# Seven block products per group in the down projection, behind a weight ring of eight

## What is computed

```python
gate, up = _split(rms_norm(x, norm_ffn[i]) @ w_gate_up[i], (D_FF, D_FF))
x = x + (jax.nn.silu(gate) * up) @ w_down[i]
```

## Time and profile before

| what | us |
|---|---|
| median of 3 runs | 2176.54 (2176.45 to 2178.01) |
| the profiled execution, own time | 2178.24 |
| its span, first to last instruction | 2176.4 |
| gate/up loop, layer 0 and 1 | 428.10, 428.33 |
| down projections, layer 0 (with the start of the next stage), layer 1 | 245.11, 239.51 |
| TensorE, VectorE, ScalarE busy in the span | 2158.2, 1555.4, 1095.3 |

### The profile page before, as it was taken

How to read it: one execution, slowest core, us unless ns; L and a number is a source line. 1 busy time by engine, 2 the same in 40 slices (tenths; PEclk the granted TensorE clock), 3 DMA queues, 4 the chain that set the end, 5 groups by cost and what they waited for, 6 DMA issues and landing times.

```text
span 2176.4 us, 29853 instructions
## 1 busy us (share of the span) xinstructions
PE 2158.2 (99%) x10052; PEld 1784.3 (82%) x10052; DVE 1555.4 (71%) x1937; ACT 1095.3 (50%) x1414; POOL 58.4 (3%) x99
## 2 busy tenths in 40 slices
PE   8999999999999999999999999999999999999999
PEld 6888888888888888888888888888878888888887
DVE  6657766888888885555566767677888888874443
ACT  7755654545555554444444444454454545544332
POOL 2101100000000000000100000000000000000000
PEclk9999999999999999999999999999999999999999
DMA  8765466667666666666555656566676666666664
GB/s 313 233 194 155 138 211 204 202 194 222 202 206 214 214 217 199 205 205 202 177 172 164 202 158 191 172 206 209 195 221 203 205 208 217 201 219 218 202 203 133
DMA packets 244569, 435.57 MB, mean 200 GB/s; under 512 B 23040, under 2 KB 43648, under 8 KB 244480
## 3 DMA queue, kind: packets, MB, share of 16 engines
q1 hardware_dynamic: 243392, 432.31, 63.7%
q10 hardware_dynamic: 1088, 2.10, 0.2%
HBM read 411.25 MB, written 2.10 MB: 190 GB/s over the span
## 4 chain that ended last, share of the span: by engine, by line
PE 70%; DVE 11%; issue 7%; SPq 6%; DMA 4%; ACT 2%; DVEq 1%; ACTq 0%
PE unit_bank L1801 52%; SPq L408 5%; PE mix_bank L1853 4%; PE mix_bank L1801 4%; DMA raw<-in_w_gate_up 4%; PE unit_bank L1853 3%; DVE w_lo L1074 3%; PE unit_bank L1813 1%; PE mix_bank L1813 1%; PE mix_bank L1871 1%; DVE sums L1096 1%; ACT w_hi L615 1%; PE mix_bank L2001 1%; DVE up_ff L1574 1%; DVE act_ff L1598 1%
## 5 line engine op out<-in xcount | busy, mean ns | idle before, releaser
L1074 DVE TENSOR_TENSOR w_lo<-raw,w_hi 128x1024 fp32r<-128x1024 f32 x687 | 828.8, 1220 | 472.8 <-ACT w_hi L615 450.7
L615 ACT ACTIVATE w_hi<-raw 128x1024 fp32r<-128x1024 f32 x687 | 719.0, 1057 | 603.4 <-PE unit_bank L1801 381.9
L1801 PE MATMUL unit_bank<-w_hi,gT_hi 128*128 128x512 f32 x704 | 217.1, 389 | 1.3 <-issue 1.3
L1801 PE MATMUL unit_bank<-w_lo,gT_hi 128*128 128x512 f32 x704 | 216.9, 389 | 0.0
L1801 PE MATMUL unit_bank<-w_hi,gT_lo 128*128 128x512 f32 x704 | 216.8, 389 | 0.0
L1801 PE MATMUL unit_bank<-w_hi,hT_hi 128*128 128x512 f32 (+1 forms) x576 | 181.2, 396 | 0.0
L1801 PE MATMUL unit_bank<-w_hi,hT_lo 128*128 128x512 f32 (+1 forms) x576 | 176.2, 387 | 0.0
L1801 PE MATMUL unit_bank<-w_lo,hT_hi 128*128 128x512 f32 (+1 forms) x576 | 175.9, 387 | 0.0
L1801 PEld LDWEIGHTS unit_bank<-w_hi,gT_hi 128*128 128x128 f32 x704 | 132.0, 188 | 29.4 <-issue 2.0
L1801 PEld LDWEIGHTS unit_bank<-w_lo,gT_hi 128*128 128x128 f32 x704 | 132.2, 188 | 27.5
L1801 PEld LDWEIGHTS unit_bank<-w_hi,gT_lo 128*128 128x128 f32 x704 | 132.2, 188 | 27.4
(11 more groups left out here) (348 smaller groups left out, 3113.9 us busy)
## 6 DMA issues: line engine op xcount, KB each, us to landing
raw<-in_w_gate_up SPq DMA_DIRECT2D x352, 512.0 KB, 4.2
raw<-in_w_down SPq DMA_DIRECT2D x176, 512.0 KB, 4.6
raw<-in_w_in_b SPq DMA_DIRECT2D x104, 512.0 KB, 4.0
raw<-in_w_o SPq DMA_DIRECT2D x64, 512.0 KB, 4.4
raw<-in_w_in_a SPq DMA_DIRECT2D x40, 512.0 KB, 3.9
moved<-turned SPq DMA_DIRECT2D x528, 32.0 KB, 2.6
raw<-in_w_mem_kv SPq DMA_DIRECT2D x31, 512.0 KB, 5.6
tanh_ff<-act_ff SPq DMA_DIRECT2D x112, 32.0 KB, 3.3
```

Source lines behind the costliest of these rows:

```text
L615: act.activation(w_hi[:, s, :, :], raw[:, s, :, :], ACT.Copy).then_inc(sems["hi_ready"], 1)
L1074: dve.tensor_tensor(w_lo[:, s, :, :], raw[:, s, :, :], w_hi[:, s, :, :].bitcast(F32), ALU.subtract).then_inc(sems["lo_ready"], 1)
L1801: ins = pe.matmul(all_banks[2 * pair + tile][:, 0:cols], stationary[part][:, kt + j, tile * P:(tile + 1) * P], b[:, s, j, 0:cols], start=o ...
```

## The change

`raw` gets eight slots (RAW), and `w_lo` is written over `raw`. SP waits for the use of a piece (`piece_used`) rather than for its low part. In the gate/up chunks the sums of a seven-product group are made from the raw pieces before they are split: DVE makes them four steps ahead (`seven_sums`), one of them in place of a block of the piece, ACT and DVE split the two pieces as any other, and the other three sums are split in the step before the group (`sums_high`, `sums_low`). The fourth product of a group no longer needs a sum that is waited for. The moved block of gT is split in step 12, its moves are issued by SP two pieces later, tanh and silu move to steps 2 and 4.

The down projection goes by two pairs of column blocks instead of four blocks. A pair has 22 quads, each two pieces (one a side); five of them, DOWN_SEVEN, take seven products. Their forms are made from gT in the steps FORM_STEPS of the first pair (`down_form`, ACT's `form_hi`, `down_form_lo`), and serve both pairs. The last five quads are done side by side: the left side's end is added at step 39, and the right side's after the last piece. `down_shared` adds the shared banks to x at step 35. Where layer 0's blocks are transposed, moved and split changes with it; block 2 is now split in step 0 of the next projection, where TensorE waits for it at piece 4. The matmuls of a group and what it reads:

```diff
+RAW = 8
...
+DOWN_SEVEN = (4, 7, 10, 13, 16)
+FORM_STEPS = (1, 9, 15, 21, 27)
...
+DOWN_ORDER = ([(q, side) for q in range(DOWN_QUADS - DOWN_SIDES) for side in range(2)]
+              + [(q, side) for side in range(2) for q in range(DOWN_QUADS - DOWN_SIDES, DOWN_QUADS)])
...
+SHARED_STEP = 2 * DOWN_SEVEN[-1] + 2
+LEFT_STEP = DOWN_PIECES - DOWN_SIDES
...
-        raw = keep("raw", [RING, 2, COLS])
...
+        raw = keep("raw", [RAW, 2, COLS])
+        w_lo = at("w_lo", [RAW, 2, COLS], F32R, place[0] - RAW * 2 * COLS * 4)
...
-        w_lo = keep("w_lo", [RING, 2, COLS], F32R)
...
-                s = slot[0] % RING
+                s = slot[0] % RAW
                 slot[0] += 1
-                t.move("lo_ready")
-                if t.any("lo_ready", RING):
-                    sp.wait_ge(sems["lo_ready"], t.value("lo_ready", RING))
+                t.move("piece_used")
+                if t.any("piece_used", RAW):
+                    sp.wait_ge(sems["piece_used"], t.value("piece_used", RAW))
...
-                chunk_turns = moves({11: (0, 6), 12: (6, 12), 13: (12, 16)})
...
+                chunk_turns = moves({13: (0, 6), 14: (6, 12), 15: (12, 16)})
...
+                    down_turns[1] = {first + n: (4 * n, 4 * n + 4) for first in (2, 15) for n in range(4)}
+                for p in range(2):
+                    for n, (q, side) in enumerate(DOWN_ORDER):
+                        piece(wd, 2 * q, (2 * p + side) * COLS)
+                        moves(down_turns[p])(n)
...
+                act.activation(w_hi[:, s, :, :], raw[:, r, :, :], ACT.Copy).then_inc(sems["hi_ready"], 1)
...
+            def sums_high(sums):
+
+                act.activation(sums.hi[:, 0:2, :], sums.two[:, :, :], ACT.Copy)
+                act.activation(sums.hi[:, 2, :], sums.all[:, :], ACT.Copy).then_inc(sems["sum_hi_ready"], 1)
...
+                        if i + LEAD in SEVEN_PIECES:
+                            act.wait_ge(sems["sum_ready"], t.next("sum_ready", 3))
+                        if i + LEAD - 2 in SEVEN_PIECES:
+                            sums_high(chunk_sums)
+                        if i == 2:
                             gate_tanh()
...
-                        if i == 14:
+                        if i == 12:
                             moved_block(gT, j * 4)
 
...
+                        if i + LEAD in DOWN_SEVEN_PIECES:
+                            act.wait_ge(sems["sum_ready"], t.next("sum_ready", 3))
+                        if i + LEAD - 2 in DOWN_SEVEN_PIECES:
+                            sums_high(down_sums)
...
+                        if p == 0 and i - 1 in FORM_STEPS:
+                            form_hi(FORM_STEPS.index(i - 1))
...
+                        if i == SHARED_STEP:
+                            act.wait_ge(sems["piece_used"], t.value("at"))
+                            act.activation(down_two[:, 0, :], shared[0][:, :], ACT.Copy).then_inc(sems["first_copied"], 1)
...
+                        added_sums(2 * p)
+                        added_sums(2 * p + 1)
...
-                t.move("split")
-                if t.any("split", RING):
-                    dve.wait_ge(sems["piece_used"], t.value("split", RING))
-                dve.tensor_tensor(w_lo[:, s, :, :], raw[:, s, :, :], w_hi[:, s, :, :].bitcast(F32),
+                dve.tensor_tensor(w_lo[:, r, :, :], raw[:, r, :, :], w_hi[:, s, :, :].bitcast(F32),
                                   ALU.subtract).then_inc(sems["lo_ready"], 1)
...
+            def seven_sums(sums):
+
+                r = (slot[0] + 1) % RAW
...
+                dve.wait_ge(sems["piece_used"], t.value("at"))
+                for n in (r, r + 1):
+                    dve.wait_ge(sems[f"arrived{n}"], t.value(f"arrived{n}", -16))
+                dve.tensor_tensor(sums.two[:, :, :], blocks[:, 1:3, :], blocks[:, 0:1, :].broadcast_to([P, 2, COLS]),
                                   ALU.add).then_inc(sems["sum_ready"], 1)
                 dve.wait_ge(sems["sum_ready"], t.next("sum_ready"))
...
+                dve.tensor_tensor(blocks[:, 0, :], sums.two[:, 1, :], blocks[:, 1, :], ALU.add).then_inc(sems["sum_ready"], 1)
                 dve.wait_ge(sems["sum_ready"], t.next("sum_ready"))
-                dve.tensor_tensor(sum_all[:, :], w_sum[:, s, 0, :], blocks[:, 3, :], ALU.add).then_inc(sems["lo_ready"], 2)
+                dve.tensor_tensor(sums.all[:, :], blocks[:, 0, :], blocks[:, 3, :], ALU.add).then_inc(sems["sum_ready"], 1)
+                t.move("sum_ready")
+
+            def sums_low(sums):
...
                 dve.wait_ge(sems["sum_hi_ready"], t.next("sum_hi_ready"))
-                dve.tensor_tensor(sums_lo[:, :, :], sums[:, :, :], sums_hi[:, :, :].bitcast(F32),
+                dve.tensor_tensor(sums.two_lo[:, :, :], sums.two[:, :, :], sums.hi[:, 0:2, :].bitcast(F32), ALU.subtract)
+                dve.tensor_tensor(sums.all_lo[:, :], sums.all[:, :], sums.hi[:, 2, :].bitcast(F32),
                                   ALU.subtract).then_inc(sems["sum_lo_ready"], 1)
...
-                    for i in chunk_pieces():
-                        if i == 1:
+                    for i in pieces(CHUNK_PIECES):
+                        if i + LEAD + 1 in SEVEN_PIECES:
+                            seven_sums(chunk_sums)
+                        if i + LEAD - 2 in SEVEN_PIECES:
+                            sums_low(chunk_sums)
+                        if i == 4:
                             gate_silu()
                         if i == 5:
                             times_up()
+                        if i == 12:
+                            moved_block(gT, j * 4, "gT_ready")
                         if i == 13:
                             shared_products(shared)
-                        if i == 14:
-                            moved_block(gT, j * 4, "gT_ready")
                     own_products(own)
 
...
+                def down_form(n):
+
+                    kt, parts = 2 * DOWN_SEVEN[n], [down_work[:, m, :] for m in range(8)]
+                    hi, lo = (g[:, kt:kt + 2, :].rearrange("p k n -> p (k n)").bitcast(F32) for g in gT)
+                    dve.tensor_tensor(down_work[:, 0:4, :].rearrange("p k n -> p (k n)"), hi, lo, ALU.add).then_inc(sems["dve_chain"], 1)
+                    dve.wait_ge(sems["dve_chain"], t.next("dve_chain"))
+                    dve.tensor_tensor(parts[4], parts[1], parts[3], ALU.subtract).then_inc(sems["dve_chain"], 1)
+                    dve.tensor_tensor(parts[7], parts[1], parts[0], ALU.subtract)
+                    dve.wait_ge(sems["dve_chain"], t.next("dve_chain"))
+                    dve.tensor_tensor(parts[5], parts[0], parts[4], ALU.subtract).then_inc(sems["dve_chain"], 1)
+                    dve.wait_ge(sems["dve_chain"], t.next("dve_chain"))
+                    dve.tensor_tensor(parts[6], parts[2], parts[5], ALU.subtract).then_inc(sems["form_ready"], 1)
...
+                def down_form_lo(n):
+
+                    dve.wait_ge(sems["hi_block"], t.next("hi_block"))
+                    hi, lo = (g[:, 2 * DOWN_SEVEN[n], P:2 * P] for g in gT)
+                    dve.tensor_tensor(down_forms[1][:, n, :, :], down_work[:, 4:7, :], down_forms[0][:, n, :, :].bitcast(F32), ALU.subtract)
+                    dve.tensor_tensor(lo, down_work[:, 7, :], hi.bitcast(F32), ALU.subtract).then_inc(sems["down_form_ready"], 1)
...
+                def down_shared(p, shared):
...
+                    dve.wait_ge(sems["first_copied"], t.next("first_copied"))
+                    dve.wait_ge(sems["piece_used"], t.value("at", 1))
+                    dve.tensor_tensor(both, shared[3][:, :], first, ALU.subtract).then_inc(sems["dve_chain"], 1)
+                    dve.tensor_tensor(x12, shared[0][:, :], x12, ALU.add)
+                    dve.tensor_tensor(x11, shared[1][:, :], x11, ALU.add)
+                    dve.tensor_tensor(x21, shared[1][:, :], x21, ALU.add).then_inc(sems["dve_chain"], 1)
+                    dve.wait_ge(sems["dve_chain"], t.next("dve_chain", 2))
+                    dve.tensor_tensor(first, shared[2][:, :], both, ALU.add).then_inc(sems["own_free"], 1)
+                    t.move("own_free")
+                    dve.tensor_tensor(x11, x11, both, ALU.add)
+                    dve.wait_ge(sems["own_free"], t.value("own_free"))
+                    dve.tensor_tensor(x21, x21, first, ALU.add)
+                    dve.tensor_tensor(x22, x22, first, ALU.subtract).then_inc(sems["dve_chain"], 1)
+                    dve.wait_ge(sems["dve_chain"], t.next("dve_chain"))
...
+                def down_own(p, side, own):
+
+                    dve.wait_ge(sems["piece_used"], t.value("at"))
+                    for s in range(TILES):
+                        part = x_tok[:, s, (2 * p + side) * COLS:(2 * p + side + 1) * COLS]
+                        dve.tensor_tensor(part, own[2 * s + side][:, :], part, ALU.add).then_inc(sems["block_added"], 1)
...
+                        if p == 0 and i == 2:
                             gate_silu()
```

(50 more changed lines are left out.)

252 lines of the change are left out of this document (111 added, 141 removed).

## The result

The changed kernel takes 2150.22 us (median of 4 runs, 2149.67 to 2150.36) against 2177.22 of the kernel before beside it (2176.45 to 2178.01). The ratio is 0.9875, 95% interval 0.9858 to 0.9893: 27.0 us less. Forecast were 2153.5 us and a gain of 23.1. The profiled executions stand at 2178.24 and 2150.24 us, 28.0 apart.

The account below looks back on a forecast made before the run. TensorE was taken as the bound everywhere. Gains of 13.0 (down projections), 8.5 (loops) and 1.6 us (seam) sum to 23.1, taking the profiled 2178.24 to 2155.1, a median of 2153.5 us; range 2149 to 2165.

Parts of the forecast that it names:

- Down projection, 13.0 forecast: Down projections of both layers: 60 matmuls fewer at 0.2268 us bring 13.6 us, less 0.6 for waits, net 13.0.
- The term of 0.03 us a group: Each new down projection group was to lose 0.03 us over the bare spacing to waits inside it, 0.6 in all.
- 8.5 + 1.6 = 10.1 forecast: Gate/up loops: 8.5 us from sums made ahead (bounds 0 and 9.9), 1.6 from the step into the down projection.
- The 12.7 that I counted as lost: Both gate/up loops: 6.25 and 6.48 us without a matmul, over 1860 matmuls at 0.2268 us each.
- The ledger of VectorE: Chunks and down projections: VectorE's work laid out against when TensorE wants each tile; chunks' smallest covers (time in hand) 0.6, 0.9 us.
- The moved block at the end of layer 0: Layer 0's last move lands 4.2 us into the next projection; loss 0, at most 1.5 us.
- The seam, 1.6: Step from loop to down projection: gT made at step 12, not 14, gains 2 x 0.8 = 1.6 us; bounds 0, 1.6.
- A: Rival: only the matmuls go, the chunks' waits stay, moved to piece 5 or 9; at 2162 us, chance 0.17.
- C: Rival: a removed down projection matmul brings less than its spacing, 7.9 us in place of 13.6; 2159 us, chance 0.03.
- D: Rival: down projection's step order fails, TensorE waits at forms or after `down_shared`, 13 us given back; 2166 to 2174, chance 0.10.
- B: Rival: VectorE becomes the bound in groups, late sums costing 40 us against the 24.7 won; 2192 us, chance 0.04.
- issued 2.3 us earlier: SP's load queue: with eight slots a load is issued some 2.3 us earlier and no longer hangs on a late VectorE.

Follow-up runs that it names:

- one group a pair: The changed kernel with one group of seven products in each pair of the down projections instead of five: 2161.29 us.
- the small dose: The changed kernel with one unused VectorE reduction of 512 elements (some 0.6 us) ahead of each group's sums: 2162.24 us.
- all steps back: The changed kernel with tanh and silu in step 1, gT's split in step 14 and the moves after pieces 11 to 13 again: 2164.01 us.
- the doses: The changed kernel with an unused VectorE reduction ahead of each group's sums, of 512 elements (2162.24 us) or 1536 elements (2207.26 us).
- the moves back: The changed kernel with only the 16 moves of a chunk's block put back after pieces 11 to 13 in SP's order: 2184.35 us.

## Why the prediction was right, and where it was off

- *TensorE is the bound everywhere.* Shown: windows with no time without a matmul in both loops and both down projections, and the slope of one group a pair.
- *Down projection, 13.0 forecast, 13.85 measured.* 60 spacings, 13.6, stand. The term of 0.03 us a group was wrong: inside the groups a wait that is met in time costs nothing, the starts stay 0.2267 apart. The 0.25 more is the seam's and was not in the sum: in the kernel before, the first ten matmuls behind the late start into each down projection come 0.125 us late together, 0.08 of it on the first step (0.305 instead of 0.227), and behind them every spacing is bare, at the borders of its four blocks too. The page "TensorE: Matmul & The Clock Gate" of the Trainium skill, section Back-to-back issue gap, has some 131 ns for a sustained pair; the slope of 226.7 disagrees and decides.
- *Loops with their seams, 8.5 + 1.6 = 10.1 forecast, 13.56 measured.* This is the term that was mis-sized, and it makes nearly the whole difference. The 12.7 that I counted as lost was itself 0.8 too low (the spacing of 0.2268 for 0.2267, and window bounds). Of it I left 1.2 as a floor of groups, which is not there, and took off another 1.4 because two covers were thin. A thin cover costs nothing as long as it holds: in this kernel all chunks but each loop's first repeat to within 0.02 us, so a discount for risk was a mean over cases that don't occur.
- *The ledger of VectorE.* Covers forecast 0.9 at piece 5 and 0.6 at piece 9; the trace has 0.9 and 0.8, and the small dose independently some 0.75. In the first pair of the down projection pieces 8 and 9 were forecast for +20 and are ready at 813.2, +19.6; piece 38 with 0.7 has 0.8. A 128-wide operation was taken at 0.29; it takes 0.28 or 0.29. Bounds from rows on both sides were good enough.
- *The moved block at the end of layer 0* was forecast 4.2 us into the next projection, without loss. ScalarE takes it at 1030.12, 3.9 after 1026.19, and TensorE has no gap there.
- *The seam, 1.6.* It is gone, but not for the reason given alone: with all steps back it did not return. So something else in the change closes it as well. In that run gT_lo ends 42.2 us after the start of layer 0's last chunk, 0.7 before TensorE starts on it, against 43.4 in the kernel before: VectorE comes to it earlier with the old step too. Which part does that was not singled out.
- *Rivals.* A fell (no wait stayed), C fell, D fell. B has the mechanism and, from the doses, a threshold: about 0.4 us of VectorE a group to the first loss, and between 0.6 and 1.7 to no gain. I had put even at 0.41 a group, which was lost time on TensorE, not work on VectorE. The 24.7 behind it is no sum of my terms; they give 23.1, or 24.5 at their upper bounds, so 0.39 to 0.41.
- *What the working left out.* The ring of eight stood in it as "issued 2.3 us earlier" and the place of the moves as cost nothing. The runs show both as conditions. Sums a step late cost the loops 27.4 us and the old place of the moves 33.7, each more than the 13.56 that the loops had gained; one piece less of lead costs the down projections 8.1, two cost the loops 49. The loops' gain has no single part that brings it: it needs the sums ahead, the lead and the place of the moves together, and is there without the new place of tanh and silu. That lead and moves came out on the good side was not worked out beforehand; there the prediction was lucky.
- *Left open.* The start is 1.02 us earlier and 0.6 of it is given back by slower matmuls: the first twelve steps are 0.43 us or more apart, against nine before. Among the kernels that share its start the first matmul lies between 7.8 and 8.6, so I don't put the 0.4 down to the change. Why the moves back cost 34 alone and 14 with gT made at step 14 was not tested further; that split comes after the late pieces in the second, which fits, but the second has tanh and silu back too. The ring of four with low parts in place and sums ahead was not tried.

## What to carry to other kernels

Where TensorE is dense, count the removed matmuls at their spacing, and lay the other engines' work out against the time at which each tile is wanted; here covers of 0.8 and 0.9 us gave the full gain, since every chunk repeats the one before. Then move each queue's slowest item in that layout by one step on paper: here a step of the sums, one piece of lead or the place of sixteen small transfers was each worth 9 to 34 us. The new order of steps, alone on the old kernel, cost 49 us: judge an order together with the ring and the placing of the sums that it was laid out for.

## What the runs showed of the hardware

A wait on TensorE that is already met costs nothing measurable: groups with two or three waits run at 226.7 ns a matmul. A wait that is met late costs its lateness, start to start, and 0.11 us on the next matmul, in the earlier trace rows as in the small dose. The idle time that the profile shows for it is shorter than the lateness (0.29 for 0.45), since the matmul before is booked to its modelled end, 0.39 after its start. A move between partitions on SP's queue takes 0.62 us to issue, six in 3.7, while a load of 512 KB takes 0.38 there. Sixteen moves hold the queue for 9.8 us in the changed kernel as well, without loss; 34 us were lost when they stood two pieces earlier, where SP waited up to 8.0 us for the transposes that they read, with the loads behind it.
